# A two-block transformer kernel on one core: another order of the first expert tiles, a gather without stride, a shorter inverse transform, and the attention output normalised ahead of the weight splits

## The reference

```python
def hier_moe(h, w_rg, b_rg, w_re, b_re, w_gate, w_up, w_down):   # 4 groups x 8 experts, top 2 of one group
    ...
    for g in range(N_GROUPS):
        hid = jax.nn.silu(jnp.einsum("bld,edf->blef", h, w_gate[g])) * jnp.einsum("bld,edf->blef", h, w_up[g])
        out = out + jnp.einsum("blef,ble,efd->bld", hid, comb[:, :, g], w_down[g])

def long_conv(u, k_spec, bias):
    L = u.shape[1]
    uf = u.astype(jnp.float32)
    y = jnp.fft.irfft(jnp.fft.rfft(uf, n=2 * L, axis=1) * k_spec[None], n=2 * L, axis=1)[:, :L]
    return (y + uf * bias.astype(jnp.float32)).astype(u.dtype)

# second_block
        for o, gate in enumerate((x1, x2)):
            zc = gate * long_conv(zc, k_spec[:, o], hy_bias[l, o])
        u_hy = (zc * jax.nn.silu(z_hy)) @ w_hy_out[l]
        ...
        attn = dense_bidirectional_attention(q, k, v_a)
        u_attn = (attn * jax.nn.silu(z_attn)) @ w_attn_out[l]
        gates = jax.nn.sigmoid(jnp.concatenate([gate_hy, gate_attn], axis=-1) + b_gate[l])
        merged = g_hy * u_hy + g_at * u_attn
        x = x + merged @ w_out[l]
```

## Time and profile before

| quantity | value |
|---|---|
| median of 3 runs | 827.77 us (826.31 to 828.32) |
| the profiled execution | 827.5 us |
| its span in the trace | 825.7 us |
| PE busy | 756.3 us, 92% |
| DVE busy | 459.6 us, 56% |
| ACT busy | 325.1 us, 39% |
| DMA moved | 190.25 MB, mean 230 GB/s |

### The profile page before, as it was taken

How to read it: one execution, slowest core, us unless ns; L and a number is a source line. 1 busy time by engine, 2 the same in 40 slices (tenths; PEclk the granted TensorE clock), 3 DMA queues, 4 the chain that set the end, 5 groups by cost and what they waited for, 6 DMA issues and landing times.

```text
span 825.7 us, 11026 instructions
## 1 busy us (share of the span) xinstructions
PE 756.3 (92%) x4622; PEld 575.5 (70%) x4622; DVE 459.6 (56%) x817; ACT 325.1 (39%) x482; POOL 17.8 (2%) x14
## 2 busy tenths in 40 slices
PE   4999999999999999989699898689999999999798
PEld 4978876878877886655245354358999765688586
DVE  5778955646866655341252131067776886645653
ACT  5554447437345323211010110056763631277421
POOL 0000000000000000000000000001100030000000
PEclk9999999999999999999899999799999999999989
DMA  9655643232458679499999999996474632432301
GB/s 318 182 202 204 204 153 103 86 108 80 137 186 320 258 306 404 171 392 420 422 420 420 421 421 421 418 354 196 125 241 153 236 123 101 146 109 103 102 0 52
DMA packets 62579, 190.25 MB, mean 230 GB/s; under 512 B 7418, under 2 KB 11772, under 8 KB 50045
## 3 DMA queue, kind: packets, MB, share of 16 engines
q1 hardware_dynamic: 60750, 184.70, 59.9%
q10 hardware_dynamic: 1774, 4.79, 1.7%
HBM read 188.43 MB, written 1.05 MB: 229 GB/s over the span
## 4 chain that ended last, share of the span: by engine, by line
PE 59%; DMA 16%; DVE 13%; ACT 8%; issue 2%; SPq 0%; POOL 0%; ACTq 0%; DVEq 0%
PE pb L511 56%; DMA raw<-in_w_exp_up 7%; DVE WL L1743 5%; ACT WH L1248 4%; PE pb L520 3%; DMA WHo<-in_w_exp_up 3%; DMA WLo<-in_w_exp_up 3%; DMA WLo<-in_w_exp_down 2%; ACT arena L1404 1%; DMA raw<-in_w_in 1%; DVE cv_ L1849 1%; DVE arena L2008 1%; ACT arena L1276 0%; POOL small L2628 0%; DVE arena L2054 0%
## 5 line engine op out<-in xcount | busy, mean ns | idle before, releaser
L1743 DVE TENSOR_TENSOR WL<-raw,WH 128x2048 fp32r<-128x2048 f32 (+5 forms) x80 | 173.4, 2177 | 97.2 <-ACT WH L1248 97.2
L1248 ACT ACTIVATE WH<-raw 128x2048 fp32r<-128x2048 f32 (+5 forms) x80 | 145.0, 1822 | 99.2 <-PE pb L511 89.7
L511 PE MATMUL pb<-WH,HTh 128*128 128x512 f32 (+2 forms) x384 | 156.7, 408 | 13.6 <-DVE HTl L1773 3.4
L511 PE MATMUL pb<-WL,HTh 128*128 128x512 f32 (+2 forms) x384 | 148.9, 388 | 0.0
L511 PE MATMUL pb<-WH,HTl 128*128 128x512 f32 (+2 forms) x384 | 148.8, 387 | 0.0
L511 PEld LDWEIGHTS pb<-WH,HTh 128*128 128x128 f32 x384 | 73.0, 190 | 33.8 <-DVE WL L1743 6.4
L511 PEld LDWEIGHTS pb<-WL,HTh 128*128 128x128 f32 x384 | 73.0, 190 | 14.7
L511 PEld LDWEIGHTS pb<-WH,HTl 128*128 128x128 f32 x384 | 73.1, 190 | 13.2 <-issue 1.0
L511 PE MATMUL pb<-arena 128*32 128x256 f32 (+6 forms) x252 | 61.5, 453 | 2.6 <-DMA arena<-in_w_exp_gate 1.9
L511 PE MATMUL pb<-WH,arenao 128*128 128x512 f32 x192 | 59.6, 392 | 1.2 <-DVE arenao L1777 1.2
L2282 DVE TENSOR_TENSOR rt_<-rt_,pb 128x256 f32<-128x256 f32 x8 | 3.4, 422 | 88.4 <-ACT rt_ L1520 88.4
(11 more groups left out here) (360 smaller groups left out, 1286.6 us busy)
## 6 DMA issues: line engine op xcount, KB each, us to landing
raw<-in_w_in SPq DMA_DIRECT2D x46, 1024.0 KB, 5.1
raw<-in_w_exp_up SPq DMA_DIRECT2D x16, 1024.0 KB, 23.3
arena<-in_w_exp_gate SPq DMA_DIRECT2D x14, 1024.0 KB, 21.6
arena<-in_w_exp_down SPq DMA_DIRECT2D x11, 1024.0 KB, 17.4
raw<-in_w_out SPq DMA_DIRECT2D x8, 1024.0 KB, 5.1
WHo<-in_w_exp_down SPq DMA_DIRECT2D x8, 1024.0 KB, 17.8
WLo<-in_w_exp_down SPq DMA_DIRECT2D x8, 1024.0 KB, 20.8
raw<-in_w_attn_out SPq DMA_DIRECT2D x6, 1024.0 KB, 5.6
```

The source lines that it names most:

```text
L511: return e.matmul(o, l, r, start=start, stop=stop, skip_group_check=True)
L1248: e.activation(h_, r_, ACT.Copy).then_inc(hi.sem, hi.mark(k))
L1743: e.tensor_tensor(l_, r_, h_.bitcast(F32), ALU.subtract).then_inc(lo.sem, lo.mark(k))
```

## The change

There are six edits.

1. **First tiles.** The first twelve expert tiles are put into the same twelve buffers in another order, by a table: buffers 0 to 11 take up 2, down 0, up 3, gate 0, gate 1, down 1, down 2, down 3, gate 2, gate 3, up 0, up 1 of q=0. Half of XG lies in buffer 6, which now holds a tile of down(0), so the gathers for q=2 and 3 all stand in q=1 now (none in q=0), and later ones are as before in number. The constants of the second block, which ACT's queue fetches at q=0, are issued after ACT's drain of down(0) rather than before it.
2. **Gather.** XNh and XNl are stored in the order that the gather wants, so its stationary slices are contiguous. The two producers (ACT xh, DVE gather_low) now read X with a step of 8 elements. The values are the same.
3. **Inverse transform.** The two frequency halves are added and subtracted on DVE first (four more 128x512 operations for each o), and PE runs two fp32 matmuls for each t in place of four. The tables ic and is_ are half as long.
4. **Banks of the fillers.** za, gate0 and gate1 alternate between banks 6, 7 and 4, 5, and everything else in the transforms uses banks 0 to 3, counted from 0.
5. **End of the attention.** The sigmoids of gates 2 and 3 leave the head loop and come after it; DVE does the last filler step of the loop without its weight split, normalises O2, and only then splits; the transposes of O2 stand two filler chunks after the loop, ahead of the rest of the filler, and its low part ahead of the last filler drains.
6. **wo2.** DVE splits the weights of the first half of wo2 ahead of the residual.

The diff, cut to its core:

```diff
@@ tile table
+        once = [("up", 0, 2), ("down", 0, 0), ("up", 0, 3), ("gate", 0, 0), ("gate", 0, 1), ("down", 0, 1), ("down", 0, 2),
...
+        moe_tiles[0:12] = once
@@ tensor
+        gathers = lambda q: () if q in (0, 6, 7) else range(4) if q == 1 else (2 * (q % 2), 2 * (q % 2) + 1)
...
-                        open_fill[name] = [ring.take((name, t), drainer, at=6 + t) for t in range(2)]
+                        open_fill[name] = [ring.take((name, t), drainer, at=fill_at[0] + t) for t in range(2)]
+                        fill_at.rotate(1)
...
-                            ins = mul(o[:, (c % 2) * 256:(c % 2) * 256 + 256], x[:, t, slice(c, c + 127 * 8 + 1, 8)],
+                            ins = mul(o[:, (c % 2) * 256:(c % 2) * 256 + 256], x[:, t, 128 * c:128 * c + 128],
...
+            ring.of, ring.i = range(4), 0
+            fill_at.append(4)
...
-                    ve.wait_ge(e, ("yf", o_, 1))
+                    ve.wait_ge(e, ("yf", o_, t))
...
-                    for mat, yy in (("ic", YR), ("is_", YI)):
-                        for f in range(2):
-                            ins = mul(o[:, :], C[mat][:, f * 256 + t * 128:f * 256 + t * 128 + 128], yy[:, f, :],
-                                      n == 0, n == 3)
+                    mul(o[:, :], C["ic"][:, t * 128:t * 128 + 128], (T0, YR[:, 0, :])[t], True, False)
+                    ins = mul(o[:, :], C["is_"][:, t * 128:t * 128 + 128], (T1, YI[:, 0, :])[t], False, True)
...
+            fill(2)
+            ve.wait_ge(e, "o2")
+            transposed("o2T", lambda t: O2[:, t, :], 4)
             fill(99)
...
-            ve.wait_ge(e, "o2")
-            transposed("o2T", lambda t: O2[:, t, :], 4)
@@ scalar
-                e.activation(XNh[:, t, :], X[:, t, :], ACT.Copy, scale=ss[:, t:t + 1]).then_inc(
+                e.activation(by_chunk(XNh[:, t, :]), every_8th(X[:, t, :]), ACT.Copy, scale=ss[:, t:t + 1]).then_inc(
...
+            for i in (2, 3):
+                sigmoid(i)
+            high("o2T", OT2, 4, after=(("gate", 3), 1))
             fill(99)
-            high("o2T", OT2, 4, after=(("gate", 3), 1))
@@ vector
+                    if f:
+                        ve.wait_ge(e, ("ys", o_, 1))
+                        e.tensor_tensor(T0, YR[:, 0, :], YR[:, 1, :], ALU.add).then_inc(ve.sem, ve.mark(("yt", o_)))
...
+                e.tensor_tensor(T1, YI[:, 0, :], YI[:, 1, :], ALU.subtract).then_inc(ve.sem, ve.mark(("yf", o_, 0)))
+                e.tensor_tensor(YR[:, 0, :], YR[:, 0, :], YR[:, 1, :], ALU.subtract)
+                ve.wait_ge(e, ("yf", o_, 0))
+                e.tensor_tensor(YI[:, 0, :], YI[:, 0, :], YI[:, 1, :], ALU.add).then_inc(ve.sem, ve.mark(("yf", o_, 1)))
...
-                fill(1)
+                fill(1, h < 10)
...
+            weights(used(("whn", 0)))
+            low("o2T", OT2, 4)
             fill(99)
-            low("o2T", OT2, 4)
...
+            weights(used(("wo2", 0)))
```

More of the change, by code:

```diff
@@ L69, in constants @@
     two["fs1"] = tile(np.sin((te[:, None] + 1) * th[None, :128]))
[L70 to L71 removed]
+    two["ic"] = np.cos(th[:128, None] * te[None, :]) / 256.0
+    two["is_"] = -np.sin(th[:128, None] * te[None, :]) / 256.0
     tt = np.linspace(0.0, 1.0, L)[:, None]
@@ L416, in program @@
                 moe_tiles += [(m, q, g) for g in range(4)]
+        once = [("up", 0, 2), ("down", 0, 0), ("up", 0, 3), ("gate", 0, 0), ("gate", 0, 1), ("down", 0, 1), ("down", 0, 2),
+                ("down", 0, 3), ("gate", 0, 2), ("gate", 0, 3), ("up", 0, 0), ("up", 0, 1)]
+        assert sorted(once) == sorted(moe_tiles[0:12])
+        moe_tiles[0:12] = once
         ring, buffer_of, held_before, held_last = deque(), {}, {}, {}
@@ L994, in tensor @@
                     mul(o[0:1, 0:1], any_, C["ones"][:, 0:1]).then_inc(mm.sem, mm.mark("over"))
-                if q < 6:
-                    gather(q // 2 + 1, 2 * (q % 2))
-                    gather(q // 2 + 1, 2 * (q % 2) + 1)
+                for j in gathers(q):
+                    gather(q // 2 + 1, j)
                 if q == 1:
@@ L1280, in drain_t, with sigmoid @@
                 e.activation(dst, pb(name)[:, 0:dst.shape[1]], ACT.Copy).then_inc(ac.sem, ac.mark(name))
+            def sigmoid(i):
+                for t in range(2):
+                    gv = G_[i // 2][:, t, (i % 2) * 512:(i % 2) * 512 + 512]
+                    ve.wait_ge(e, (("gate", i), t))
+                    e.activation(gv, gv, ACT.Sigmoid).then_inc(ac.sem, ac.mark((("gate", i), t)))
             def filled(name, c):
@@ L1305, in filled @@
                     drain(name, ZA, ACT.Silu, by=rg)
-                elif name[0] == "gate":
-                    for t in range(2):
-                        gv = G_[i // 2][:, t, (i % 2) * 512:(i % 2) * 512 + 512]
-                        ve.wait_ge(e, (name, t))
-                        e.activation(gv, gv, ACT.Sigmoid).then_inc(ac.sem, ac.mark((name, t)))
+                elif name[0] == "gate" and i < 2:
+                    sigmoid(i)
                 weights(used(key))
```

67 lines of the change are left out of this document (34 added, 33 removed).

## The result

The changed kernel takes 813.66 us (median of 4 runs, 812.5 to 816.31), the kernel before, on the same chip, 828.05 us (826.31 to 828.35). The ratio is 0.983, with a 95% interval of 0.980 to 0.986. The forecast was 812.9 us, 0.8 us lower. Its profiled execution took 816.31 us, the longest of the four, with a span of 814.5 us.

What follows compares the result with a forecast made beforehand. DMA was taken to bound the experts, with idle engines just ahead, and PE what follows. Savings of 6.2, 1.7 and 6.7 us sum to 14.6, from 827.5 to 812.9 us; own range 810.5 to 815.5, overall 809 to 819.5.

Steps and rivals of the forecast that it cites:

- the three terms: Savings at first tiles and gather 6.2 us, the middle 1.7 us and the end of the attention 6.7 us.
- First tiles and gather: Expert start: idle DMA time falls from 11.2 to 5.0 us, gate(0) starts at 329.8, saving 6.2 us.
- The factor of 1.77 for strided reads: Gather's producers: strided reads on ACT and DVE cost 1.77 times, as in weight loads; each DVE read 2.3 us.
- the rival that made it four times: Gather: strided reads cost four times, 10.3 us stay idle, only 0.9 us saved, 818.2 us; chance 0.13.
- The rival of the constants: Second block's constants come behind queued tiles, PE stops in q=1, up to 6.2 us idle returns: 819.1 us; chance 0.10.
- The middle: From 655.87 to 717.19: 3.7 us earlier less 2.0 us of cold clock, saving 1.7 us.
- it would go on at 713.5 instead of 717.19, 3.7 us earlier: At the uT transposes: PE waits some 3.7 us for DVE, yet goes on 3.7 us earlier than before.
- the new wait at the first forward transform: First forward transform: its first matmul waits for a bank that ACT empties, adding 2.8 us.
- edits 3 and 4 may bring only new waits: Middle saves 0, attention's end 2.9 us, first tiles 6.2 us, giving 818.4 us; chance 0.06.
- The end of the attention: Around wa2: 3.8 us earlier start, 2.0 us less cold clock, 0.86 us wait gone, saving 6.7 us.
- I had let wa2 wait for DVE's low part till 780.7: At wa2: DVE makes the low part by 780.4, wa2 starts at 780.7 instead of 784.48, 3.8 us earlier.

Runs made afterwards that it cites:

- e7: The changed kernel with the ring of banks 0 to 3 starting at bank 1: 811.7 us.
- e10: The changed kernel with O2 normalised and transposed late again, sigmoids still behind the loop: 820.55 us.
- e4: The changed kernel with four matmuls for each half of the inverse transform again, no sums and differences on DVE: 813.39 us.
- e5: The changed kernel with all fillers back in banks 6 and 7 and the others in banks 0 to 5: 815.3 us.
- e8: The changed kernel with the bank ring starting at bank 1 and eight matmuls for each inverse transform again: 810.71 us.
- e2: The changed kernel with the old tile order, gathers back in q=0 and constants ahead of the drain of down(0): 819.85 us.
- e3: The changed kernel with XNh and XNl stored straight, strided stationary slices and dense reads by ACT and DVE: 817.25 us.
- e6: The changed kernel with the attention's end undone: sigmoids in the head loop, O2 normalised behind the split, transposes behind the filler: 819.5 us.
- e9: The changed kernel with the sigmoids of gates 2 and 3 back in the head loop, early O2 normalisation kept: 814.76 us.
- e1_after: The changed kernel itself, unaltered, timed again on another chip beside the kernel before: 813.2 us.

## Why the prediction was right, and where it was not

The time is within 0.1% of the forecast, and the three terms were in the right places. Their sizes were not all right: two of the errors cancelled, and the profiled executions saved 2 to 3 us less than the medians. That the total came out to 0.1% is luck; that the three places together bring 11 to 14 us is not.

*First tiles and gather, forecast 6.2 us.* In the execution with a warm gather every step came out: gate(0) at 329.76 (forecast 329.8), idle DMA time 5.0 us (5.0), last tile 6.5 us earlier (6.2). The factor of 1.77 for strided reads, taken from the weight loads, lies between DVE's 1.61 and ACT's 1.93, and ACT ended at 321.82, hidden as forecast. The Trainium skill's rule of 16-byte lines ("SBUF — State Buffer", section "Specifications (TRN2)") is right in direction; the rival that made it four times (each DVE read 5.1 us) is refuted by the 2.06 us row. What was missing is the clock, at two places. In the first profile the pause of 1.24 us in front of the gather is followed by half clock, which costs 1.3 us (PE was busy for 0.89 of the 2 us from 323 to 325; in the kernel before, with a pause of 0.46 us, for 1.54, and the clock stayed). And down(7), the last product of the stage, runs at half clock behind its waits for DMA in both profiles of the change (matmuls of 1.06 and 1.00 us in place of 0.62), so from the last tile to the end of the experts it takes 6.9 us where 5.2 was. The stage gave 3.6 and 4.8 us. Of the eleven executions that waited 1.4 to 1.5 us for the last tile, four ran it at half clock (the change twice, e7, e10) and seven did not, so this too is a loss that comes and goes.

*The rival of the constants* came as PE's wait of 8.8 us, but not its price, for the reason named against it: with 21 buffers in flight the DMA share of after stays between 1.00 and 1.02 from 348 to 400 us. The forecast took the full rate for that stretch, though, and it was 404 GB/s in after where 409 was before.

*The middle, forecast 1.7 us.* This is the step that failed: "it would go on at 713.5 instead of 717.19, 3.7 us earlier". The transposes came only 1.6 us earlier relative to the beginning of the middle (59.7 against 61.3 us). I counted the new wait at the first forward transform with its length of 2.8 us and took the matmuls behind it at full clock; the eight ran in 8.83 instead of 7.03 us, and DVE's products, which wait for them, moved by the same 1.8 us. I had priced a cold stretch behind one wait and not behind the other. That this is the step is shown by the two executions in which the transform stayed warm: there the middle took 58.0 us, 3.3 less than before, against the 3.7 of the forecast. So the order of the waits and DVE's row were right to 0.4 us, and the missing cold stretch is the other 1.7. The stretch behind the transposes cost 2.6 us (102.3 against 99.7 us to the end, e4, e5, e8) where I had 2.0 us. So the middle, with what it does to the clock behind it, was 1.0 us slower than before, not 1.7 faster. The rival "edits 3 and 4 may bring only new waits" described it, with a chance of 0.06; e4_inverse_back shows it for edit 3, and e8_bank1_inverse shows that the two edits stood in each other's way.

*The end of the attention, forecast 6.7 us.* From the transposes to the end it took 102.3 us in place of 108.5, 6.2 less, and with the 2.6 us of cold clock that belong to the middle taken out 8.8 less. I had let wa2 wait for DVE's low part till 780.7. DVE had it ready at 774.92 + 1.28 = 776.2 in the trace of after, and PE came at 776.67, held up by its own matmuls, so the whole wait of 3.40 us went, and the 1.31 us and most of the 0.45 us with it; I had built ACT's and DVE's rows on the loop's old end and so let the 1.3 us that the loop itself gains drop out. The two misses, 2.7 us too much in the middle and 2.1 too little here, nearly cancel.

*Sum.* The profiled spans fell by 11.2 and 12.4 us, the medians by 14.4. The nine executions of the change in the two sessions have spans from 810.1 to 814.5 us, and the two that were profiled are the longest of their sessions. By that the terms above, read from two profiles, account for 2 to 3 us less than the medians show; which stage the shorter executions gain them in was not recorded. The candidate is the three cold stretches that come and go: the gather 1.3 us, the last tile 1.7, the first transform 1.7. Both profiled executions had the last two. That the shorter ones lacked them is not shown; the mean granted clock of a run doesn't tell (0.964 at 810.1 us, 0.969 at 812.8).

## What to carry to other kernels

Where work moves from the bound engine to another, draw the other engine's row through the same stretch first: here eight matmuls saved on PE bought eight operations on a DVE with no slack, and undoing that costs nothing, while undoing it together with one bank number gives about 3 us (2.7 by the medians, 3.1 to 4.8 by the profiles). The ring of buffers gave its gain by which tile sits in a buffer that comes back first, at no cost in bytes or instructions. And price each new wait of TensorE with the slow matmuls that can follow it, not only with its length: here that was another 1.3 to 2.6 us each, where it came.

## What the runs showed that I had not expected

The same wait does not always bring the same clock. With the 2.6 us in front of the first forward transform, eight executions of it were profiled (the change twice, e2, e3, e4, e6, e9, e10): six ran the transform in 8.83 us and two, e6_tail_back and e9_sigmoids_back, in 7.13. Five of the eight (the change twice, e6, e9, e10) have the same instructions up to there, and both kinds are among them. With the 1.24 us in front of the gather it was six at half clock of eleven, with the 1.4 to 1.5 us in front of the last expert tile four of eleven. Behind the 4.25 us in front of the transposes it came in all eight executions that had it, in e3_stride_back for a shorter time (1.23 us for the transposes, not 1.98). So one profile can be off by 1.3 to 1.7 us for each such place, and a forecast of this size should give each of them a chance.

A strided fp32 read (32 bytes apart, 128x1024) cost 1.61 times on DVE, where it is one of two inputs, 1.93 times on ACT, where it is the only one, and, as weight load of TensorE (128x128), 336 ns in place of 190. And with the DMA share at 1.0 the rate fell from 420 GB/s to 275 over 10 us in e2_order_back, where the second block's constants moved together with expert tiles (363 and 365 in e1_after).
